# Output projection of the mixed rows by seven block products instead of eight

## The reference

```python
mixed = (gates[:, :, 0] * (out_a @ w_o_nsa[l]) + gates[:, :, 1] * (out_b @ w_o_mla[l])
         + gates[:, :, 2] * (out_c @ w_o_fox[l]))
x = x + mixed.astype(x.dtype) @ w_out[l]
x = x + hier_moe(rmsnorm(x, norm_ffn[l]), ...)
```

## Time and profile before

| | |
|---|---|
| three runs | 1013.55, 1018.01, 1015.57 us; median 1015.57 |
| profiled execution | 1014.46 us, span from its first to its last instruction 1012.5 us |
| TensorE (PE) busy | 936.8 us, 93% of the span, mean granted clock 0.971 |
| VectorE busy | 383.2 us, 38% |
| ScalarE busy | 241.6 us, 24% |
| GpSimd busy | 78.6 us, 8% |
| DMA | 295.14 MB, mean 291 GB/s |
| `w_out` matmuls, L2109 | 256 instructions of 128x256, 58.2 us busy in both layers |
| TensorE idle before L2206 (experts' gate and up) | 46.6 us, 42.5 of it for a DMA |

### The profile page before, as it was taken

The page is one execution under the profiler, slowest core; times in us unless marked ns, Lnnn a source line. Parts: engine busy times, 40 slices in busy tenths (PEclk is TensorE's granted clock), DMA queues, the critical chain, the costliest instruction groups (busy, mean ns, idle before and its releaser), DMA issues. The chain is left out here.

```text
span 1012.5 us, 14003 instructions
## 1 busy us (share of the span) xinstructions
PE 936.8 (93%) x5512; PEld 638.8 (63%) x5512; DVE 383.2 (38%) x1034; ACT 241.6 (24%) x682; POOL 78.6 (8%) x121
## 2 busy tenths in 40 slices
PE   9999999999999998677899999999999999986676
PEld 8888778775586543334288887887747855532342
DVE  2523676774633211111131337677565321100112
ACT  1211454552111020000111015655411202000002
POOL 0300000114000000000020000000220000000000
PEclk9999999999999998898999999999999999987899
DMA  9985655439989999999998443436398999999995
GB/s 291 299 271 143 139 168 160 167 99 316 333 353 361 421 420 421 422 421 421 359 311 268 130 149 111 143 100 220 122 358 310 351 402 417 420 422 420 421 415 186
DMA packets 137191, 295.14 MB, mean 291 GB/s; under 512 B 14158, under 2 KB 101412, under 8 KB 115620
## 3 DMA queue, kind: packets, MB, share of 16 engines
q1 hardware_dynamic: 132672, 289.41, 77.5%
q10 hardware_dynamic: 4452, 4.81, 2.5%
HBM read 291.56 MB, written 2.64 MB: 291 GB/s over the span
## 5 line engine op out<-in xcount | busy, mean ns | idle before, releaser
L2206 PE MATMUL bank<-ring,tail 128*32 128x512 f32 x896 | 113.5, 664 | 46.6 <-DMA ring<-in_moe_w_up 42.5
L1266 PE MATMUL bank<-ring,tail 128*128 128x256 f32 x672 | 156.3, 384 | 0.2
L1266 PEld LDWEIGHTS bank<-ring,tail 128*128 128x128 f32 x672 | 124.3, 190 | 24.5 <-issue 8.3
L1074 PE MATMUL bank<-tail,ring 128*128 128x256 f32 x512 | 112.6, 380 | 0.0
L2206 PEld LDWEIGHTS bank<-ring,tail 128*32 128x32 f32 x896 | 32.6, 121 | 123.3 <-issue 123.1
L1074 PEld LDWEIGHTS bank<-tail,ring 128*128 128x128 f32 x512 | 96.7, 190 | 13.3 <-issue 0.4
L2507 DVE SCALAR_TENSOR_TENSOR tail<-tail,bank 128x256 f32<-128x256 f32 x16 | 6.7, 422 | 232.1 <-ACT tail L2356 232.1
L1602 ACT ACTIVATE ring<-ring,small 128x128 f32<-128x128 f32 (+1 forms) x128 | 56.6, 444 | 77.4 <-DVE small L1896 77.4
L1428 PE MATMUL bank<-ring,tail 128*128 128x512 f32 x168 | 73.6, 594 | 0.0
L2263 PE MATMUL bank<-ring,tail 128*32 128x512 f32 x480 | 60.3, 610 | 7.7 <-DMA ring<-in_moe_w_down 4.1
L2213 PE MATMUL bank<-tail 128*128 128x512 f32 x128 | 59.2, 606 | 0.0
(11 more groups left out here) (334 smaller groups left out, 1155.5 us busy)
## 6 DMA issues: line engine op xcount, KB each, us to landing
ring<-in_moe_w_up SPq DMA_DIRECT2D x56, 1024.0 KB, 22.6
ring<-in_moe_w_gate SPq DMA_DIRECT2D x56, 1024.0 KB, 20.6
ring<-in_moe_w_down SPq DMA_DIRECT2D x52, 1024.0 KB, 15.2
ring<-in_w_in SPq DMA_DIRECT2D x47, 1024.0 KB, 9.0
ring<-in_w_out SPq DMA_DIRECT2D x8, 1024.0 KB, 8.5
ring<-in_moe_w_down SPq DMA_DIRECT2D x16, 512.0 KB, 15.9
ring<-in_moe_w_gate SPq DMA_DIRECT2D x14, 512.0 KB, 8.9
ring<-in_moe_w_up SPq DMA_DIRECT2D x14, 512.0 KB, 9.1
```

The costliest lines, as they stand in the source:

```text
L1074: last = pe.matmul(dst, weight(k), hT[:, k, :], start=(k == 0), stop=(k == KD - 1))
L1266: last = pe.matmul(dst, tokens[:, k, :], weights[:, k, :], start=False, stop=(k == KD // 2 - 1), skip_group_check=True)
L2206: last = pe.matmul(bank[4][CAP * e:CAP * e + CAP, :].rearrange("p (a f) -> p a f", a=2), XT[:, k, CAP * e:CAP * e + CAP], ring[:, lo:hi + ...
```

## The change

The output projection becomes seven block products as well. The mixed rows are four blocks of 128 tokens by 512 inputs (a11, a12 of token half 0, a21, a22 of half 1), `w_out` four blocks of 512 by 512 (left_top, left_low, right_top, right_low), and each is loaded as a block. Each product is four matmuls of 512 columns; the fourth is made in two halves of 256.

- SP: the same number of loads. The four `w_out` loads have 2 KB rows; loads 16, 18, 19, 20 wait for other things and come in the order 19, 20, 16, 18.
- GpSimd: right_top - left_top (128x2048) at the end of its attention part, once both have landed; later left_low - right_low' in four pieces of 128x512.
- VectorE: four token sums; right_low - right_top and right_low' - left_top in four pieces each, while the third and the sixth product use up the old values; nine residual additions, six of 512 columns and three of 256, for eight of 256.
- ScalarE: three copies from bank to bank (running sums), and one copy less of a turned block, since VectorE forms the sums straight from bank 3.
- TensorE: the products in the order 1, 2, 5, 3, 6, 7, 4; the second half of the tokens is transposed and meets the router in another order of its columns.

```diff
-            i = n - L_OUT
-            whole(A["w_out"][layer].rearrange("(k p) n -> p k n", k=KD)[:, :, 256 * i:256 * i + 256])
+            right, low = divmod(n - L_OUT, 2)
+            w = A["w_out"][layer].rearrange("(k p) n -> p k n", k=KD)
+            sp.dma_start(ring[:, att_slot(n), :].rearrange("p (k n) -> p k n", k=4),
+                         w[:, 4 * low:4 * low + 4, 512 * right:512 * right + 512]).then_inc(done, 16)
...
+    Q1, Q2, Q5, Q3, Q6, Q7, Q4A, Q4B = 1, 2, 3, 3, 8, 9, 10, 11
+    q_sum = kept(6144, KD // 2, P)
...
-            sp.wait_ge(s_op, 4)
+            sp.wait_ge(s_tp, q_made(2, 3))
+            moe_load(sp, layer, 19)
+            sp.wait_ge(s_op, Q6)
             last_extra_row(sp, layer, 0)
-            for i, c in enumerate((16, 18, 19, 20)):
-                sp.wait_ge(s_op, 5 + i)
-                moe_load(sp, layer, c)
+            sp.wait_ge(s_tp, q_made(3, 3))
+            sp.wait_ge(s_gbd, q_low_done(3))
+            moe_load(sp, layer, 20)
+            sp.wait_ge(s_op, Q7)
+            moe_load(sp, layer, 16)
+            sp.wait_ge(s_op, Q4B)
+            moe_load(sp, layer, 18)
...
+            att_wait(pool, L_OUT)
+            att_wait(pool, L_OUT + 2)
+            pool.tensor_tensor(q_weights(2), q_weights(2), q_weights(0), ALU.subtract).then_inc(s_gbd, 1)
...
-            for i in range(4):
+            for i in range(3):
                 _kind, n, t, b = TURNED[i]
                 act.wait_ge(s_mxt, i + 1)
                 act.activation(mixT[:, t, 4 * n:4 * n + 4, :],
                                bank[b][:, :].rearrange("p (k c) -> p k c", k=4), ACT.Copy).then_inc(s_mxe, 1)
+                if i == 1:
+                    act.wait_ge(s_op, Q1)
+                    act.wait_ge(s_mgd, row_done(4, 1))
+                    act.activation(bank[7][:, :], bank[4][:, :], ACT.Copy).then_inc(s_seed, 1)
...
+            pool.wait_ge(s_op, Q2)
+            low, right_low = q_weights(1), q_weights(3)
+            for k in range(4):
+                pool.wait_ge(s_tp, q_made(2, k))
+                pool.tensor_tensor(low[:, k, :], low[:, k, :], right_low[:, k, :], ALU.subtract).then_inc(s_gbd, 1)
...
+            left_top, left_low, right_top, right_low = [q_weights(i) for i in range(4)]
+            a11, a12, s3, a22 = mixT[:, 0, 0:4, :], mixT[:, 0, 4:8, :], mixT[:, 1, 0:4, :], mixT[:, 1, 4:8, :]
+            def steps(dst, tokens, weights, start, ks=range(4)):
+                for k in ks:
+                    last = pe.matmul(dst, tokens[:, k, :], weights[:, k, :], start=(start and k == 0), stop=(k == 3),
+                                     skip_group_check=True)
+                return last
+            def first_product(ks):
+                att_wait(pe, L_OUT)
+                pe.wait_ge(s_mxe, turned_mix(0, 0))
+                last = steps(bank[4][:, :], a11, left_top, True, ks)
...
+            def second_product(ks):
+                att_wait(pe, L_OUT + 1)
+                pe.wait_ge(s_mxe, turned_mix(1, 0))
+                pe.wait_ge(s_seed, q_copied(0))
+                last = steps(bank[4][:, :], a12, left_low, False, ks)
...
+            def fifth_product():
+                pe.wait_ge(s_hs, q_summed(1))
+                pe.wait_ge(s_gbd, q_top_done())
+                steps(bank[5][:, :], q_sum, right_top, True).then_inc(s_op, 1)
+            def third_product():
+                att_wait(pe, L_OUT + 3)
+                pe.wait_ge(s_hs, q_summed(4))
+                for k in range(4):
+                    steps(bank[6][:, :], a12, right_low, True, (k,)).then_inc(s_op, 1)
+            def sixth_product():
+                pe.wait_ge(s_seed, q_copied(0))
+                for k in range(4):
+                    pe.wait_ge(s_tp, q_made(2, k))
+                    last = steps(bank[7][:, :], a11, right_low, False, (k,))
+                last.then_inc(s_op, 1)
+            def seventh_product(ks):
+                pe.wait_ge(s_seed, q_copied(1))
+                for k in ks:
+                    pe.wait_ge(s_tp, q_made(3, k))
+                    last = steps(bank[7][:, :], s3, left_top, False, (k,))
+                if 3 in ks:
+                    last.then_inc(s_op, 1)
+            def fourth_product(half):
+                c = slice(256 * half, 256 * half + 256)
+                if half == 0:
+                    pe.wait_ge(s_xa, 4)
                 else:
+                    pe.wait_ge(s_seed, q_copied(2))
+                for k in range(4):
+                    pe.wait_ge(s_gbd, q_low_done(k))
+                    last = pe.matmul(bank[6 + half][:, c], a22[:, k, :], left_low[:, k, c],
+                                     start=(half == 0 and k == 0), stop=(k == 3), skip_group_check=True)
+                last.then_inc(s_op, 1)
...
-            w_out(0, 0, range(0, 4))
-            w_out(0, 1, range(0, 4))
+            first_product(range(4))
+            turn_mixed(pe, 1)
             out_piece(pe, 7, 2)
-            pe.wait_ge(s_mgd, row_done(4, 1))
-            w_out(0, 2, range(0, 4))
-            turn_mixed(pe, 1)
-            w_out(0, 3, range(0, 4))
+            second_product((0, 1))
             out_piece(pe, 4, 2)
-            w_out(0, 0, range(4, 8))
-            w_out(0, 1, range(4, 8))
             turn_mixed(pe, 2)
+            second_product((2,))
             turn_mixed(pe, 3)
-            w_out(0, 2, range(4, 8))
-            w_out(0, 3, range(4, 8))
-            w_out(1, 0)
-            pe.wait_ge(s_xa, 4)
+            second_product((3,))
+            fifth_product()
+            third_product()
+            sixth_product()
+            pe.wait_ge(s_xa, 1)
             turn_x(0, 0, range(0, 4))
+            seventh_product((0,))
+            pe.wait_ge(s_xa, 5)
             turn_x(0, 1, range(4, 8))
-            w_out(1, 1)
+            seventh_product((1, 2, 3))
             pe.wait_ge(s_wrg, 1)
             pe.wait_ge(s_xta, 1)
             pe.wait_ge(s_xtd, 1)
             logits(0)
-            w_out(1, 2)
+            fourth_product(0)
             pe.wait_ge(s_xa, 6)
-            turn_x(1, 2, range(0, 4))
+            turn_x(1, 2, range(4, 8))
+            fourth_product(1)
...
-            act.wait_ge(s_xa, 4)
-            act.activation(junk, x[:, 0, :], ACT.Square, accum_out=ss[:, 0:1]).then_inc(s_ss2, 1)
+            act.wait_ge(s_op, Q6)
+            act.wait_ge(s_xa, 1)
+            act.activation(bank[4][:, :], bank[7][:, :], ACT.Copy).then_inc(s_seed, 1)
             act.wait_ge(s_xt, 1)
             act.activation(hT[:, 0:4, 0:P], bank[0][:, :].rearrange("p (k t) -> p k t", k=4), ACT.Copy).then_inc(s_xta, 1)
+            act.wait_ge(s_xa, 5)
+            act.activation(junk, x[:, 0, :], ACT.Square, accum_out=ss[:, 0:1]).then_inc(s_ss2, 1)
+            act.wait_ge(s_op, Q7)
+            act.activation(bank[5][:, :], bank[7][:, :], ACT.Copy).then_inc(s_seed, 1)
...
-            for i in range(4):
-                add_out(0, i)
-            add_out(1, 0)
+            a11, a12, a22 = mixT[:, 0, 0:4, :], mixT[:, 0, 4:8, :], mixT[:, 1, 4:8, :]
+            a21 = bank[3][:, :].rearrange("p (k c) -> p k c", k=4)
+            dve.wait_ge(s_mxt, 4)
+            dve.wait_ge(s_mxe, 3)
+            dve.tensor_tensor(q_sum, a21, a22, ALU.add).then_inc(s_hs, 1)
+            dve.tensor_tensor(mixT[:, 1, 0:4, :], a11, a21, ALU.subtract).then_inc(s_hs, 1)
+            dve.wait_ge(s_op, Q1)
+            dve.wait_ge(s_hs, q_summed(3))
+            dve.tensor_tensor(a11, q_sum, a11, ALU.subtract).then_inc(s_hs, 1)
+            dve.wait_ge(s_op, Q2)
+            dve.wait_ge(s_hs, q_summed(2))
+            dve.tensor_tensor(a12, a12, a11, ALU.subtract).then_inc(s_hs, 1)
+            add_out(0, 0, 512, 4)
+            dve.wait_ge(s_op, Q5)
+            add_out(0, 512, 1024, 5)
+            add_out(1, 512, 1024, 5)
+            left, right, right_low = q_weights(0), q_weights(2), q_weights(3)
+            dve.wait_ge(s_gbd, q_top_done())
+            for k in range(4):
+                dve.wait_ge(s_op, Q3 + k + 1)
+                dve.tensor_tensor(right_low[:, k, :], right_low[:, k, :], right[:, k, :], ALU.subtract).then_inc(s_tp, 1)
+            dve.wait_ge(s_xa, 2)
+            add_out(0, 512, 1024, 6)
+            def third_difference(k):
+                dve.wait_ge(s_tp, q_made(2, k))
+                dve.tensor_tensor(left[:, k, :], right_low[:, k, :], left[:, k, :], ALU.subtract).then_inc(s_tp, 1)
+            third_difference(0)
+            third_difference(1)
+            dve.wait_ge(s_seed, q_copied(1))
+            dve.wait_ge(s_xa, 4)
+            add_out(0, 512, 1024, 4)
+            third_difference(2)
+            third_difference(3)
             dve.wait_ge(s_xt, 2)
             dve.tensor_copy(hT[:, 4:8, 0:P], bank[1][:, :].rearrange("p (k t) -> p k t", k=4)).then_inc(s_xtd, 1)
-            add_out(1, 1)
+            dve.wait_ge(s_seed, q_copied(2))
+            add_out(1, 512, 1024, 5)
+            add_out(1, 0, 256, 5)
```

(68 more changed lines are left out.)

31 lines of the change are left out of this document (19 added, 12 removed).

## The result

| | before | changed |
|---|---|---|
| median | 1014.96 us (5 runs, 1011.65 to 1018.01) | 1025.46 us (5 runs, 1024.09 to 1028.10) |
| profiled execution, span | 1014.46, 1012.5 us | 1024.98, 1023.2 us |
| TensorE busy | 936.8 us | 935.8 us |
| VectorE busy | 383.2 us | 416.7 us |
| GpSimd busy | 78.6 us | 100.0 us |

The account below looks back on a forecast made before the run. TensorE was taken to set the pace up to the experts' load stream, and so the end. Two layers at +2.1 us plus 2.0 us of clock made +6.2: 1021.8 us against the median, range 1012.5 to 1026.5.

Parts of the forecast that it names:

- The gain of 3.5 us: Output projection on TensorE: matmul time per layer falls from 27.65 to 24.10 us, 3.5 us gained.
- the waits of 1.9 us: TensorE's waits among the projection's new steps, every engine at its old speed: together 1.9 us per layer.
- The port: Merge products: GpSimd's 128x2048 step holds the port shared with VectorE, so TensorE stands still; 3.1 us per layer charged.
- with the longer rows of three blocks about 1.2 us sooner: Third w_out block in layer 1: lands at 759.7 instead of 760.9, which sets when GpSimd's long step starts.
- the bound that the prediction gave for the later landing, 4.3: Port charge per layer if the third block's landing stays at 760.9: up to 4.3 us.
- The duration of the 128x2048 step: GpSimd's long subtraction, estimated at 4.5 us from its steps of 256, 512 and 1024 columns.
- The short differences: GpSimd's four 128x512 steps alternate with VectorE's, mostly under the sixth and seventh products; 0.6 us per layer, at most 1.9.
- The clock: TensorE loses its clock after the new 2.9 us wait; 2.0 us charged in one of the two layers.
- TensorE to the end, one for one: Whatever moves TensorE at 811 moves the start of the full load stream and the end equally, in each layer.
- The sum per layer: Matmul gain less waits, plus port and short differences: -1.6 + 3.1 + 0.6 = +2.1 us per layer.

Follow-up runs that it names:

- e4: Changed kernel with GpSimd's five differences made on one column alone, every wait and order kept; 1009.95 us, ratio 0.9965 to the kernel before.
- e8: Changed kernel, long difference by VectorE, the four short ones on GpSimd only behind VectorE's last difference; 1010.74 us, ratio 0.9964 to the kernel before.
- e5: Changed kernel with the 128x2048 difference and the four 128x512 ones all made by VectorE; 1009.47 us, ratio 0.9954 to the kernel before.
- e1: Kernel before plus one GpSimd step per layer, multiplying a 128x2048 slot by ones, which the projection waits for; 1023.36 us, ratio 1.0094 to the kernel before.
- e3: Changed kernel with the four 128x512 differences made by VectorE, the 128x2048 one still by GpSimd; 1021.30 us, ratio 1.0075 to the kernel before.
- e6: Changed kernel with GpSimd's 128x2048 difference cut into eight pieces of 128x256 at the same place; 1017.95 us, ratio 1.0037 to the kernel before.
- e7: Changed kernel with GpSimd's 128x2048 difference started only behind the row of the sixth branch product; 1013.45 us, ratio 0.9992 to the kernel before.

## Why the prediction was right, and where its sizes were off

- **The gain of 3.5 us and the waits of 1.9 us**: right. e4 gives 1.70 us per layer for their difference, 1.6 was forecast. The terms one by one were not measured.
- **The port**: the right mechanism, the right engine and the right place (the VectorE step behind the landing of the third block, the wait ahead of the sixth branch product). The size was 3.1, measured 4.17 us. The step that failed is the landing "with the longer rows of three blocks about 1.2 us sooner". In layer 1 the third block landed 9.0 us after its issue, as before, and in layer 0 9.0 for 9.3. Its issue did not move either: it lies 11.8 us ahead of the first turn in both kernels (758.08 and 769.90, 751.88 and 763.71), because SP stands there until a branch product has released the slot (2.4 us before, 2.7 after). What the first two blocks gained was thus of no use to the third. GpSimd starts 2.69 us ahead of the turn, and the bound that the prediction gave for the later landing, 4.3, is what came. The duration of the 128x2048 step, estimated at 4.5 us, was 4.52. (The trace before has two GpSimd steps over the 2.35 us that the prediction calls the longest, 2.46 us at 711.51 and 2.54 at 213.21; the estimate does not hang on them.)
- **The short differences**: forecast 0.6, at most 1.9; measured 1.45 us. They delay VectorE's second and third differences, as said: four second ones take 4.63 us, in e8 2.06 + 0.69; two third ones take 2.83 us, in e8 1.28.

```profile
793.66 4.63 DVE L2579 TENSOR_TENSOR ring<-ring 128x512 f32<-128x512 f32 x4
...
798.81 2.83 DVE L2585 TENSOR_TENSOR ring<-ring 128x512 f32<-128x512 f32 x2
...
794.48 6.61 POOL L2113 TENSOR_TENSOR ring<-ring 128x512 f32<-128x512 f32 x4 [22.76 <-DVE ring L2579]
```

  The term is too small because the sixth and seventh products were taken as cover for most of it. The transposes of the second four blocks of columns stand between them and wait for the residual row behind these steps; that wait is 1.03 us here and is gone in e5 and e8.
- **The clock**: forecast 2.0 us once; 1.1 us in layer 0 behind the wait, none in layer 1. With some 1.3 us behind the gathers the clock cost about what was charged, but that is luck: the second part was not foreseen, and e5 has its like without the wait. In e1 both layers lost it. Of the six waits of 3.0 to 3.7 us of the changed kernel, e1 and e3, four show a granted clock under 1.00 in the matmuls behind them, and two (layer 1 of the changed kernel and of e3) do not. What decides is open.
- **TensorE to the end, one for one**: right. The sums of both stage lengths, less those of before, are +8.9, +9.8, -0.5, +5.5, -3.4, -3.4, +4.8, -0.5 and -2.9 us in the order of the table; the ratios times 1014 give +11.0, +9.5, -1.2, +7.6, -3.5, -4.7, +3.8, -0.8 and -3.7. All the stage sums lie within the intervals of the ratios save that of e3, which is 0.6 us outside; its stages come from an execution 3.4 us under its median. So the stream hid or multiplied nothing that these intervals can show.
- The sum per layer was -1.6 + 3.1 + 0.6 = +2.1, and is -1.70 + 4.17 + 1.45 = +3.92 us. With the clock that is 8.9 us in the profiled execution; the remaining 1.8 us at the first experts of layer 0 are not settled by these runs. Of the 4.5 us by which the profiled span outgrew the forecast (10.7 for 6.2), the port has 2.1, the short differences 1.7 and the first experts 1.8; the clock behind the wait was charged 0.9 too much, what was left of the gain 0.2 too little.

The Trainium skill's exclusive lock, held for the whole instruction (SBUF — State Buffer, Who interferes with whom), is borne out by the long step: a VectorE step started at 767.39 was held until the 4.52 us GpSimd step was over. In e6 VectorE steps lost 0.2 to 0.5 us beside pieces of 0.72, less than a whole piece, which the trace does not explain. The Trainium skill's warning that offloading between the two might not help (Perfetto Trace Analysis, Optimizing Scalar/DVE Operations) holds for the place taken here, where it cost more than the matmuls saved; e7 shows that at another moment the same offload costs the stage no more than VectorE doing it itself.

## What to carry to other kernels

Before work is put on GpSimd, look at which VectorE steps lie in the stretch in which it may start, and how much slack their readers have: a long two-input step cost nearly its whole duration here (4.17 of 4.52 us), and its start is set by whatever it waits for (a landing). Give such a step a semaphore of the work that it must not disturb, cut it up, or give it to VectorE, which did it in half the time (2.28 us). A saving of matmuls is worth what the new waits leave of it: here 1.7 of 3.5 us per layer, and only once GpSimd's steps were out of VectorE's way (e5).

## What the runs showed of the hardware

- GpSimd's two-input float32 step of 128x2048 takes 4.52 us, and 3.81 us where one input is 128 columns repeated 16 times; VectorE takes 2.28 us for the first.
- With both engines at work on small steps both lose: eight GpSimd steps of 128x256, 0.72 us each when alone, took 9.81 us in all, and VectorE's 128x1024 differences 1.63 to 1.74 us in place of 1.22. VectorE steps with one input in a bank kept their 0.68 us (e6).
- Weight blocks with 2 KB rows landed little sooner after their issue than columns with 1 KB rows. In layer 1, before and changed: 5.4 and 5.0 us for the first, 8.0 and 7.4 for the second, 9.0 and 9.0 for the third, 12.6 and 11.3 for the fourth.
- After a wait of 3.0 to 3.7 us TensorE ran slow in four of six cases. In layer 0 of the changed kernel the granted clock was 0.50 from 271 to 273 us, its lower level (1.2 GHz), and 1.00 (2.4 GHz) again from 274 us; in layer 1 it stayed at 1.00 behind the same wait.
